# Two layers of a hybrid backbone on one core: value-weight sums in other memory, modulation in fourteen couples, a shorter plan for the first merge

## The chip, the cores and the metric

The kernel runs on one core of a Trainium2 chip. The time is that of the device in microseconds, a median of runs. The engines are TensorE (PE, its weight loads PEld), VectorE (DVE), ScalarE (ACT), GpSimd (POOL) and SyncE (SP), which here only issues DMAs. They run their own programs and meet at semaphores.

## The reference

Two layers work on 256 latent tokens and 256 context tokens of width 1024, all in float32. Cut to what the change touches:

```python
mod_x = s_c @ w_ada[l] + b_ada[l]             # modulation: six vectors of 1024, for tokens and for context
hx = rms_norm(x, norm1_g[l]) * (1 + scx1) + shx1
px = hx @ w_in[l]                             # one combined projection: r k v ... of RWKV, q k v of attention, mLSTM, gates
ya, yb, yc = rwkv_mix(...), na_mix(...), mlstm_mix(...)
merged = ga * (ya @ w_branch[0]) + gb * (yb @ w_branch[1]) + gc * (yc @ w_branch[2])
x = x + gx1 * (merged @ w_out)
x = x + gx2 * moe_ffn(...)                    # 64 experts, 8 of them for each token
```

`wkv_scan` in the RWKV mixer is a recurrence over tokens; the kernel computes it in chunks of 64 tokens and in both directions.

## The kernel before

The stages of a layer run one behind the other, each in its own block, which ends when all engines are through: start or combine, projection (`stage_projection`), attention, mLSTM, RWKV features, scan (`stage_rwkv_scan`), readout, merge (`stage_merge`), norm, experts. SP issues the loads of a stage in a written order.

**Projection.** The weights come in 10 blocks of 1024x512 through a ring of two (`win_ring`). A block holds two couples of tiles. A couple of tiles times all 512 tokens is done by seven products of half size (Strassen's scheme in Winograd's form) where plain products would be eight: `PRODUCTS` is their order, p1, p2, p6, p7, p4, p5, p3. A product is four matmuls of 128x256 in the code, eight records in the trace; PE goes on through six PSUM banks (`NB` in the first layer; `free` waits until a bank is read). Left operands are sums of weight tiles (`left_sums`, four DVE instructions of 128x512, two sets kept in `left`), right ones sums of the activations (`right_sums`, four of 128x1024, in `right`). p1 and p2 need no sums; PE waits for them ahead of the third product (L716 to L721). Blocks 8 and 9 hold the value weights of attention and mLSTM, whose result is wanted with tokens on the partitions: there the roles turn, the token tiles are the left side (`token_sums`, eight instructions, into `token`) and the weights the right one (`feature_sums`, four instructions, into `right` for block 8 and into `left`'s room for block 9). DVE also adds the products (L834 to L852), seven adds a couple. ScalarE copies p1 (L747).

In the first layer the projection also computes eight blocks of modulation on DVE (`accumulate`, L778): a piece is one of the eight row tiles of a 1024x512 block, two instructions of 128x512 (context and token vector) and a drain, 64 pieces in all. The 16 couples of blocks 0 to 7 (`by_weights`) take four pieces each: one third behind p2's add, one behind p7's, the rest at the couple's end behind the left sums (L857). The weights of modulation alternate between `token`'s room and that of `vna` and `vml` (`halves`). When a block is summed, PE folds it with `modulate` (L686) a couple later, ScalarE copies a row, PE turns it (`turn`, L695) and DVE writes it into `k.mod` (`finish`). `acc` holds the sums of two blocks. The order of DVE's work in couple 15, after its adds: its last pieces, `token_sums`, `feature_sums(8)` (L859 to L862).

**Scan.** For each direction d there are four PSUM banks. At the start PE transposes the values, 128 tokens at a time (`values`, L2093), into bank 2 (`psV`), ScalarE copies them out (L1872), and PE waits for all four copies (L2232) ahead of `matrices`, which write banks 0, 1 and the second half of 2 (L2104, L2109). DVE copies them under a mask (`first_factor` L2013, `masks` L2034); POOL has to have cleared and filled the target first (`filled`, L1953, L1955). Then come the levels of a blockwise inverse (`level`). Bank 3 (`psR`, `psU`, `psY`) is first written inside level 1.

**Merge.** For each of the eight column tiles m, PE computes three gate products (those not done ahead) and three branch products; DVE multiplies and adds them into `mg`; behind that come eight output products (L2565). In the first layer the twelve modulation blocks of the second layer are computed in the gaps: `merge_plan` (L2363) lays down at fixed costs which pieces DVE does behind each tile and behind which product PE does `modulate` and `turn` of a block. Blocks turned ahead of the output products (`in_loop`, here 9) use the banks of `psO`, the others those of `psG`; so the first output product waits for `finish` of the last of them (L2561).

Of the kernel before, what the change touches and what calls it, by code (L numbers as in the profile page):

```python
# [16 lines left out]
ALU = mybir.AluOpType  # L17
# [517 lines left out]
def right_sums(dve, out, b):  # L535

    dve.tensor_tensor(out[:, 0], b(0, 1), b(0, 0), ALU.subtract)
    dve.tensor_tensor(out[:, 2], b(1, 1), b(0, 1), ALU.subtract)
    dve.drain()
    dve.tensor_tensor(out[:, 1], b(1, 1), out[:, 0], ALU.subtract)  # L540
    dve.drain()
    return dve.tensor_tensor(out[:, 3], out[:, 1], b(1, 0), ALU.subtract)


def operands_of(name, a, left, b, right):

    return {"p1": (lambda: (a(0, 0), b(0, 0))), "p2": (lambda: (a(0, 1), b(1, 0))), "p3": (lambda: (left[:, 3], b(1, 1))),
            "p4": (lambda: (a(1, 1), right[:, 3])), "p5": (lambda: (left[:, 0], right[:, 0])),
            "p6": (lambda: (left[:, 1], right[:, 1])), "p7": (lambda: (left[:, 2], right[:, 2]))}[name]()


def stage_projection(nc, k, l, h, pr, pn, vna, vml):
# [40 lines left out]
    per_unit = -(-NA * KD // len(by_weights))  # L593
    summed_in = [by_weights[(KD * (a + 1) - 1) // per_unit] for a in range(NA)]

    with ExitStack() as ctx:
# [20 lines left out]

        def ada_part(a, c):
            return halves[a % 2][c // HK][:, c % HK]
# [13 lines left out]
        def sides(u):  # L633

            pair, j, m = units[u]
            if j < 8:
                return w_tile(j, m), left[:, pair_of[u] % 2], h_part, right
            return h_tile(m), token[:, m // 2], w_part(j), right if j == 8 else right9
# [13 lines left out]
        with nc.Block(no_gpsimd_drain=True) as block:  # L652
# [103 lines left out]
            def _(dve):  # L756
# [16 lines left out]
                def feature_sums(j):  # L773
                    dve.wait_ge(win_in[j % 2].sem, win_in[j % 2].at(j // 2 * 16 + 16))
                    dve.wait_ge(done.sem, done.at(first_done[by_weights[-1]] + 7))
                    right_sums(dve, right if j == 8 else right9, w_part(j)).then_inc(rights.sem, 1)
# [32 lines left out]
                right_sums(dve, right, h_part).then_inc(rights.sem, 1)  # L809
# [11 lines left out]
                for u, (pair, j, m) in enumerate(units):  # L821
                    p, q, n = pair_of[u], first_done[u], 4 * j + m
                    if pair:
                        own, one = tmp[:, p % 2], p1[:, p % 2]
                        pieces = [p * per_unit + i for i in range(per_unit)] if j < 8 else []
# [33 lines left out]
                        if NA and u == by_weights[-1]:  # L859
                            token_sums()  # L860
                        if u == by_weights[-1]:
# [911 lines left out]
def stage_rwkv_scan(nc, k, l, pr, pn, sg, aa, kk, ka, y, h):  # L1773
# [21 lines left out]
    with ExitStack() as ctx:  # L1795
# [31 lines left out]
        psV = [ps[d][:, 2] for d in range(2)]  # L1827
# [26 lines left out]
        with nc.Block(no_gpsimd_drain=True) as block:  # L1854
# [230 lines left out]
            def _(pe):  # L2085
# [74 lines left out]
                def between(d, n, m):  # L2160
# [4 lines left out]
                    elif m == 1:  # L2165
                        w(pe, d, "state", n)
                        pe.wait_ge(sem[d]["yout"].sem, sem[d]["yout"].at(y_read(n)))
# [64 lines left out]
                pe.wait_ge(values_out.sem, values_out.at(NV))  # L2232
# [130 lines left out]
def merge_plan(blocks, m0):  # L2363
# [3 lines left out]
    for m in range(KD):  # L2367
# [4 lines left out]
        for b in range(3):  # L2372
            now += BRANCH
            hooks.append((now, ("branch", m, b)))
# [6 lines left out]
    on_pe = {at: [] for _, at in hooks + [last]}  # L2381
# [1312 lines left out]
```

## Time and profile before

| | |
|---|---|
| median of the runs | 2557.25 us (3 runs, 2554.91 to 2565.0) |
| the profiled execution | 2556.32 us, span 2554.5 us |
| PE busy | 2233.2 us, 87% |
| PE weight loads busy | 1587.9 us, 62% |
| DVE busy | 1292.5 us, 51% |
| ACT busy | 674.9 us, 26% |
| POOL busy | 406.9 us, 16% |

The first projection lies from 42 to 308 us of the span, the first scan from 534, the first merge's last branch products around 905 and its output products from 913; the second layer's scan begins at 1882. Busy time doesn't count semaphores and branches. A row of the timeline is a run of like instructions, and the brackets name the idle time ahead of it and what ended it. The granted clock is a share of 2.4 GHz: 1.00 is that level, 0.50 is 1.2 GHz.

### The profile page before, as it was taken

To read this page: it belongs to the slowest core of one execution; us is meant where nothing else is said; L and a number is where in the kernel's file an instruction comes from. 1 tells how busy PE (TensorE), PEld (TensorE's weight loads), DVE (VectorE), ACT (ScalarE), POOL (GpSimd) and SP (SyncE) were. 2 spreads that over 40 slices of the span, in tenths; PEclk is the share of its full clock that TensorE was granted. 3 is DMA by queue.
4 is the path that set the end of the run, shared out by engine and by line. 5 is a ranking of instruction groups with operands and counts; after the bars stand their busy time and mean duration, and the time that the engine had idled before them with its cause. 6 is when DMAs were issued, how large, how long until landed. Compare 5 with 4: busy or idle time off the path is not lost. (4 is left out here: it accounts for less than half of the span.)

```text
span 2554.5 us, 47659 instructions
## 1 busy us (share of the span) xinstructions
PE 2233.2 (87%) x18986; PEld 1587.9 (62%) x18986; DVE 1292.5 (51%) x2881; ACT 674.9 (26%) x1533; POOL 406.9 (16%) x489
## 2 busy tenths in 40 slices
PE   6999889889899998898898589999879978888885
PEld 4887765458844444565565578877658867655453
DVE  5888364676558876442122653344667532531113
ACT  2000155454430003132222110034454431122220
POOL 0000000235500001232221000000234400222210
PEclk9999999999999998999999899999989998898998
DMA  8443001100067524899896822222310052899994
GB/s 353 164 166 132 34 1 60 75 35 4 4 233 282 175 93 167 320 419 398 348 359 234 358 111 99 99 76 94 104 33 4 4 211 101 348 414 376 384 380 174
DMA packets 83245, 474.31 MB, mean 186 GB/s; under 512 B 17617, under 2 KB 29521, under 8 KB 52049
## 3 DMA queue, kind: packets, MB, share of 16 engines
q1 hardware_dynamic: 54704, 394.66, 39.6%
q0 software_dynamic: 28320, 76.60, 8.1%
q8 instruction: 153, 2.51, 0.4%
q14 instruction: 68, 0.55, 0.1%
HBM read 439.99 MB, written 61.08 MB: 196 GB/s over the span
## 5 line engine op out<-in xcount | busy, mean ns | idle before, releaser
L3007 PE MATMUL xp_psG<-moe_ring,rt_xt 128*64 128x256 f32 (+1 forms) x2048 | 331.3, 410 | 42.7 <-DMA moe_ring<-in_moe 38.8
L3007 PEld LDWEIGHTS xp_psG<-moe_ring,rt_xt 128*64 128x64 f32 (+1 forms) x2048 | 228.6, 165 | 123.4 <-issue 63.1
L3264 DVE TENSOR_TENSOR rt_sg<-rt_sg,xp_psG 128x128 f32<-128x128 f32 x84 | 24.2, 288 | 356.7 <-ACT rt_sg L3081 356.7
L3028 PE MATMUL xp_psY<-moe_ring,rt_aT 128*64 128x512 f32 (+1 forms) x512 | 161.9, 602 | 1.6 <-DVE rt_aT L3271 1.6
L724 PE MATMUL win_ps<-win_right,win_left 128*128 128x256 f32 x600 | 138.0, 380 | 2.3 <-DVE win_left L532 2.3
L724 PEld LDWEIGHTS win_ps<-win_right,win_left 128*128 128x128 f32 x600 | 113.7, 190 | 19.0 <-DVE win_left L532 2.7
L1223 POOL MEMSET ml_w<- 128x1536 f32 x4 | 5.4, 1376 | 736.4 <-POOLq L922 736.4
L2619 DVE SCALAR_TENSOR_TENSOR pr<-pr,cv_silu 128x512 f32<-128x512 f32 x168 | 118.7, 748 | 4.9 <-DMA pr<-in_ada 0.6
L2139 PE MATMUL sc_ps<-sc_NT,sc_XI 64*64 64x64 f32 x2560 | 109.4, 227 | 9.1 <-DVE sc_XI L2019 4.8
L3075 ACT ACTIVATE rt_xt<-xp_psT 128x512 f32<-128x512 f32 x168 | 90.9, 595 | 95.2 <-PE xp_psT L2992 95.1
L2134 PE MATMUL sc_ps<-sc_XI,sc_NT 64*64 64x64 f32 x2048 | 106.6, 227 | 6.2 <-issue 3.0
L2881 POOL DMA_INDIRECT y_rows<-rt_y,rt_dst x56 | 56.1, 1002 | 300.5 <-PE xp_psT L2992 207.2
L2019 DVE TENSOR_TENSOR sc_XI<-sc_ps,cst 128x256 f32<-128x256 f32 x160 | 67.5, 422 | 71.0 <-PE sc_ps L2139 69.5
L3081 ACT ACTIVATE rt_sg<-xp_psG 128x128 f32<-128x128 f32 x84 | 23.3, 277 | 288.8 <-PE xp_psG L3007 288.8
L2992 PEld LDWEIGHTS xp_psT<-cst,rt_xg 128*128 128x128 f32 x512 | 58.1, 143 | 63.9 <-issue 35.2
L724 PE MATMUL win_ps<-h,win_ring 128*128 128x256 f32 x400 | 93.0, 386 | 5.4 <-PEq L292 5.4
L2134 PEld LDWEIGHTS sc_ps<-sc_XI,sc_NT 64*64 64x64 f32 x2048 | 82.8, 135 | 18.7 <-issue 9.3
L3028 PEld LDWEIGHTS xp_psY<-moe_ring,rt_aT 128*64 128x64 f32 (+1 forms) x512 | 51.7, 153 | 66.7 <-issue 60.7
L2139 PEld LDWEIGHTS sc_ps<-sc_NT,sc_XI 64*64 64x64 f32 x2560 | 85.9, 134 | 11.3 <-DVE sc_XI L2019 6.3
L2565 PE MATMUL mg_psO<-mg_m,mg_wo 128*128 128x512 f32 (+1 forms) x256 | 85.6, 493 | 5.3 <-DVE scratch L2636 3.5
L1878 ACT ACTIVATE sc_NT<-sc_ps 128x256 f32<-128x256 f32 x160 | 61.4, 384 | 106.6 <-PE sc_ps L2139 104.8
L2992 PE MATMUL xp_psT<-cst,rt_xg 128*128 128x128 f32 x512 | 69.9, 281 | 21.1 <-DMA rt_xg<-h_rows,rt_tok 21.1
(551 smaller groups left out, 4569.3 us busy)
## 6 DMA issues: line engine op xcount, KB each, us to landing
moe_ring<-in_moe SPq DMA_DIRECT2D x128, 1536.0 KB, 14.1
win_ring<-in_win SPq DMA_DIRECT2D x20, 2048.0 KB, 8.2
pr<-in_ada POOLq DMA_DIRECT2D x24, 1024.0 KB, 5.6
cb_yg<-y_rows SPq DMA_DIRECT2D x16, 1024.0 KB, 11.8
mg_ring<-in_mg SPq DMA_DIRECT2D x16, 768.0 KB, 4.5
win_token<-in_ada SPq DMA_DIRECT2D x8, 1024.0 KB, 7.9
mg_wo<-in_wo SPq DMA_DIRECT2D x2, 4096.0 KB, 15.0
pr<-y_rows SPq DMA_DIRECT2D x8, 1024.0 KB, 17.7
```

Source lines behind the costliest of these rows:

```text
L724: last = pe.matmul(ps[:, (q + f) % NB, 0:256], x[:, c], y[:, c], start=c == 0, stop=c == HK - 1)
L1878: act.activation(NT[d][:], psWT[d], ACT.Copy).then_inc(sem[d]["wtout"].sem, 1)
L2019: dve.tensor_tensor(XI[d][:], psW[d], level_mask(d, m), ALU.mult).then_inc(sem[d]["xi"].sem, 1)
L2134: pe.matmul(psW[d][to:to + HD, hp], wt, x, start=True, stop=True)
L2139: last = pe.matmul(out[to:to + HD], x, wt, start=True, stop=True)
L2565: last = pe.matmul(psO[:, m % 2, 0:N], wo[:, c, m * P:(m + 1) * P], mg[:, c, t0:T], start=c == 0, stop=c == KD - 1)
L2619: last = dve.scalar_tensor_tensor(out=acc[:, a % 2, s], in0=slot[:, c], scalar=weight, in1=acc[:, a % 2, s], op0=ALU.mult, op1=ALU.add)
L2881: pool.indirect_dma_start(k.d_y[0:N * TOP_K], bass.IndirectOffsetOnAxis(ap=dst[:, column(u)], axis=0), y_rows[u % OUT], None, bounds_check ...
L2992: last = pe.transpose(psT[:, u % 2, c], xg[u % AHEAD][:, c * P:(c + 1) * P], k.cst("ident"))
L3007: last = pe.matmul(psG[at:at + m, u % 2, 0:2 * P].rearrange("p (q n) -> p q n", q=2), xt[:, u % 2, c, at:at + m], ring[:, slot, c:2 * KD:K ...
L3028: last = pe.matmul(psY[at:at + m, q], aT[:, u % 2, at:at + m], ring[:, slot, 2 * KD + 4 * q:2 * KD + 4 * q + 4], start=True, stop=True)
L3075: last = act.activation(xt[:, u % 2, q * 4:q * 4 + 4], psT[:, u % 2, q * 4:q * 4 + 4], ACT.Copy)
```

## The change

It has three parts. First, the 64 pieces of modulation go to the first 14 couples (4 or 5 each, `shares`) and none to couples 14 and 15, so that blocks are summed in couples 1, 3, 5, 6, 8, 10, 12 and 13 where it was every second couple to 15. In the first layer the right sums of block 8 are written to the room of `acc` and of the front of `vml` (`right8`) and not to `right`; they wait for the last `modulate` (`ada_done`) and not for couple 15's products. The token sums stand behind couple 14's work, the feature sums of block 8 behind couple 15's. Second, in the scan of both layers `psV` is bank 3, and the wait for the four copies stands ahead of the first write of bank 3 in level 1. Third, in `merge_plan` the branch products of the last column tile carry no modulation. Worked out with the plan's own costs, in the first layer modulate and turn of block index 8 move from the last tile's first and second branch product to output products 0 and 1, those of 9, 10 and 11 each one product later (turn of 11 to output product 7), `in_loop` becomes 8, `finish(8)` moves from behind the last column tile to behind output product 1. The second layer's merge has no modulation and stays as it is.

```diff
--- before.py
+++ after.py
@@ -534,19 +534,19 @@
-    dve.tensor_tensor(out[:, 0], b(0, 1), b(0, 0), ALU.subtract)
-    dve.tensor_tensor(out[:, 2], b(1, 1), b(0, 1), ALU.subtract)
+    dve.tensor_tensor(out[0], b(0, 1), b(0, 0), ALU.subtract)
+    dve.tensor_tensor(out[2], b(1, 1), b(0, 1), ALU.subtract)
     dve.drain()
-    dve.tensor_tensor(out[:, 1], b(1, 1), out[:, 0], ALU.subtract)
+    dve.tensor_tensor(out[1], b(1, 1), out[0], ALU.subtract)
     dve.drain()
-    return dve.tensor_tensor(out[:, 3], out[:, 1], b(1, 0), ALU.subtract)
+    return dve.tensor_tensor(out[3], out[1], b(1, 0), ALU.subtract)
...
     return {"p1": (lambda: (a(0, 0), b(0, 0))), "p2": (lambda: (a(0, 1), b(1, 0))), "p3": (lambda: (left[:, 3], b(1, 1))),
-            "p4": (lambda: (a(1, 1), right[:, 3])), "p5": (lambda: (left[:, 0], right[:, 0])),
-            "p6": (lambda: (left[:, 1], right[:, 1])), "p7": (lambda: (left[:, 2], right[:, 2]))}[name]()
+            "p4": (lambda: (a(1, 1), right[3])), "p5": (lambda: (left[:, 0], right[0])),
+            "p6": (lambda: (left[:, 1], right[1])), "p7": (lambda: (left[:, 2], right[2]))}[name]()
@@ -590,8 +590,9 @@
-    per_unit = -(-NA * KD // len(by_weights))
-    summed_in = [by_weights[(KD * (a + 1) - 1) // per_unit] for a in range(NA)]
+    EARLY = 14
+    shares = [range(NA * KD * i // EARLY, NA * KD * (i + 1) // EARLY) if i < EARLY else range(0) for i in range(len(by_weights))]
+    summed_in = [by_weights[next(i for i, x in enumerate(shares) if KD * (a + 1) - 1 in x)] for a in range(NA)]
@@ -615,6 +616,14 @@
+        if NA:
+            flat_acc = acc[:].rearrange("p a s n -> p (a s n)").rearrange("p (f c n) -> p f c n", f=2, c=HK)
+            flat_vml = vml[:].rearrange("p a h v -> p (a h v)")[:, 0:HK * 512].rearrange("p (f c n) -> p f c n", f=2, c=HK)
+            right8 = [flat_acc[:, 0], flat_acc[:, 1], flat_vml[:, 0], flat_vml[:, 1]]
+        else:
+            right8 = [right[:, f] for f in range(4)]
+        early = NA > 0
+
         def ada_part(a, c):
@@ -634,8 +643,8 @@
             if j < 8:
-                return w_tile(j, m), left[:, pair_of[u] % 2], h_part, right
-            return h_tile(m), token[:, m // 2], w_part(j), right if j == 8 else right9
+                return w_tile(j, m), left[:, pair_of[u] % 2], h_part, [right[:, f] for f in range(4)]
+            return h_tile(m), token[:, m // 2], w_part(j), right8 if j == 8 else [right9[:, f] for f in range(4)]
@@ -772,8 +781,11 @@
                     dve.wait_ge(win_in[j % 2].sem, win_in[j % 2].at(j // 2 * 16 + 16))
-                    dve.wait_ge(done.sem, done.at(first_done[by_weights[-1]] + 7))
-                    right_sums(dve, right if j == 8 else right9, w_part(j)).then_inc(rights.sem, 1)
+                    if j == 8 and early:
+                        dve.wait_ge(ada_done.sem, ada_done.at(NA))
+                    else:
+                        dve.wait_ge(done.sem, done.at(first_done[by_weights[-1]] + 7))
+                    right_sums(dve, right8 if j == 8 else [right9[:, f] for f in range(4)], w_part(j)).then_inc(rights.sem, 1)
@@ -806,7 +818,7 @@
-                right_sums(dve, right, h_part).then_inc(rights.sem, 1)
+                right_sums(dve, [right[:, f] for f in range(4)], h_part).then_inc(rights.sem, 1)
                 weight_sums(0)
@@ -822,7 +834,7 @@
                         own, one = tmp[:, p % 2], p1[:, p % 2]
-                        pieces = [p * per_unit + i for i in range(per_unit)] if j < 8 else []
+                        pieces = list(shares[p]) if j < 8 else []
                         a, b = len(pieces) // 3, 2 * len(pieces) // 3
@@ -856,9 +868,11 @@
                             accumulate(i)
-                        if NA and u == by_weights[-1]:
+                        if early and u == by_weights[-2]:
                             token_sums()
-                        if u == by_weights[-1]:
+                        if early and u == by_weights[-1]:
+                            feature_sums(8)
+                        if not early and u == by_weights[-1]:
                             feature_sums(8)
@@ -1824,7 +1838,7 @@
         psA2 = [[half(d, 2, 1)[o * HD:(o + 1) * HD] for o in range(2)] for d in range(2)]
-        psV = [ps[d][:, 2] for d in range(2)]
+        psV = [ps[d][:, 3] for d in range(2)]
         psBK = [ps[d][:, 2] for d in range(2)]
@@ -2164,6 +2178,8 @@
                         w(pe, d, "state", n)
+                        if n == 0:
+                            pe.wait_ge(values_out.sem, values_out.at(NV))
                         pe.wait_ge(sem[d]["yout"].sem, sem[d]["yout"].at(y_read(n)))
@@ -2229,7 +2245,6 @@
                     values(j)
-                pe.wait_ge(values_out.sem, values_out.at(NV))
                 for d in range(2):
@@ -2371,14 +2386,15 @@
             now += BRANCH
-            hooks.append((now, ("branch", m, b)))
+            if m < KD - 1:
+                hooks.append((now, ("branch", m, b)))
         ends.append(now)
...
     last = (now + 3.0, ("end", 0, 0))
-    on_pe = {at: [] for _, at in hooks + [last]}
+    on_pe = {at: [] for _, at in hooks + [last] + [(0.0, ("branch", KD - 1, b)) for b in range(3)]}
     turned = []
...
```

## Rows read from the trace of the kernel before

**Rows 1.** What PE waited for, one of its rows: us in total, times, longest.

```profile
PE win_ps L724 <- DVE win_right L542: 10.6, 1, 10.6
```

**Rows 2.** Timeline of PE at block 8: start us, us, engine, line, operation.

```profile
245.84 3.62 PE L724 MATMUL win_ps<-win_ring,h 128*128 128x256 f32 x16
260.00 5.49 PE L724 MATMUL win_ps<-win_right,win_token 128*128 128x256 f32 x16 [10.55 <-DVE win_right L542]
```

**Rows 3.** Timeline of DVE in the same stretch.

```profile
246.27 2.89 DVE L792 SCALAR_TENSOR_TENSOR win_acc<-vml,cv_silu,win_acc 128x512 f32<-128x512 f32 x4
...
254.90 1.22 DVE L537 TENSOR_TENSOR win_right<-win_ring 128x1024 f32<-128x1024 f32 x1
```

**Rows 4.** Windows: busy time (and instructions) by engine, granted clock, DMA share, GB/s.

```profile
260.00:264.00 4.00, 4.00 (x10) 3.25 (x11) 0.69 (x3) 0.00 (x0) 0.00 (x0) 0.54 0.02 4
...
912.70:915.40 2.70, 2.64 (x3) 1.17 (x4) 1.24 (x2) 0.00 (x0) 0.00 (x0) 0.50 0.00 0
```

**Rows 5.** Timeline of PE behind two other idles, projection and second merge.

```profile
49.44 3.72 PE L724 MATMUL win_ps<-win_right,win_left 128*128 128x256 f32 x16 [2.33 <-DVE win_left L532]
...
2131.54 27.86 PE L2565 MATMUL mg_psO<-mg_m,mg_wo 128*128 128x256 f32 x128 [1.77 <-DVE mg_m L2658]
```

**Rows 6.** Projection, couples 3 to 12: window, DVE's waits, starts of couples.

```profile
104.60:214.20 109.60, 109.60 (x574) 94.23 (x573) 96.28 (x196) 4.84 (x14) 0.00 (x0) 1.00 0.47 173
...
DVE pn L852 <- PE win_ps L724: 4.4, 5, 1.0
DVE pr L852 <- PE win_ps L724: 1.3, 2, 1.0
...
95.52 3.62 PE L724 MATMUL win_ps<-h,win_ring 128*128 128x256 f32 x16
...
120.68 3.62 PE L724 MATMUL win_ps<-h,win_ring 128*128 128x256 f32 x16
...
95.61 0.42 DVE L852 TENSOR_TENSOR pr<-win_ps,win_tmp 128x256 f32<-128x256 f32 x1 [0.97 <-PE win_ps L724]
...
104.64 0.42 DVE L834 TENSOR_TENSOR pr<-win_ps,win_p 128x256 f32<-128x256 f32 x1
...
115.91 0.42 DVE L834 TENSOR_TENSOR pr<-win_ps,win_p 128x256 f32<-128x256 f32 x1
```

**Rows 7.** Timeline of the first layer's scan from its start.

```profile
536.62 2.33 PE L2093 MATMUL sc_ps<-cst,pr 128*128 128x128 f32 x8 [0.66 <-ACT sc_uv L1872]
540.27 2.08 PE L2104 MATMUL sc_ps<-sc_ra,sc_hat 64*128 64x128 f32 x16 [1.32 <-ACT sc_uv L1872]
...
537.85 0.61 DVE L1940 TENSOR_TENSOR sc_hat<-sc_kd,sc_rise 128x256 f32<-128x256 f32 x1
...
541.50 0.62 DVE L1940 TENSOR_TENSOR sc_hat<-sc_kd,sc_rise 128x256 f32<-128x256 f32 x1
543.52 0.90 DVE L2013 COPY_PREDICATED pn<-cst,sc_ps 64x256 f32<-64x256 uint32 x2 [1.41 <-PE sc_ps L2109]
```

**Rows 8.** Timeline of the second layer's scan.

```profile
1893.72 1.42 POOL L1953 COPY h<-cst 64x256 f32<-64x256 f32 x4 [8.73 <-issue]
...
1895.40 0.89 DVE L2013 COPY_PREDICATED pn<-cst,sc_ps 64x256 f32<-64x256 uint32 x2 [6.63 <-POOL scratch L1955]
```

**Rows 9.** Timeline of the first layer's merge, last branch products and output products.

```profile
905.67 3.60 PE L2548 MATMUL mg_psY<-pn,mg_ring 128*128 128x512 f32 x8
912.76 15.38 PE L2565 MATMUL mg_psO<-mg_m,mg_wo 128*128 128x512 f32 x32 [3.49 <-DVE scratch L2636]
928.07 0.62 PE L2510 MATMUL mg_psG<-pr,mg_pick 128*2 128x128 f32 x16
928.61 7.13 PE L2565 MATMUL mg_psO<-mg_m,mg_wo 128*128 128x512 f32 x16
...
935.69 7.03 PE L2565 MATMUL mg_psO<-mg_m,mg_wo 128*128 128x512 f32 x16
...
910.92 0.69 DVE L2658 TENSOR_TENSOR mg_m<-mg_gateb 128x512 f32<-128x512 f32 x1
```

## The prediction

> **What bounds the kernel now.** I read the engine shares first (the table above), then what TensorE (PE) waited for, then the timelines around the three places that the change touches. PE is busy for most of the span, but a share doesn't price an edit: the stages run one behind the other, so a stage gets shorter only where PE, or the chain that feeds it, waits less. PE's waits in reach of the diff are 10.6 us before the third product of the first projection's block 8 [rows 1], 3.5 us before the first output product of the first layer's merge [rows 9], and 1.3 us in the first layer's scan before the first matrices [rows 7]. Of the rest nothing is edited but the like place in the second layer's scan. The prize is below 20 us, and the question is how much of each wait another wait takes over.
>
> **Part A, the first projection.** 64 pieces of modulation go into 14 couples of tiles instead of 16 (4 or 5 a couple, none in the last two), and the sums for block 8 (the token sums, and `feature_sums(8)` into `right8`) move ahead.
>
> What is removed. After the last add of couple 15, VectorE (DVE) does two pieces (246.27), then the token sums, then the four feature sums (254.90) [rows 3]. PE does block 8's first two products, which need no sums, until 245.84+3.62=249.46 and goes on at 260.00, 10.55 us idle [rows 2]. In the changed kernel pieces and token sums are gone from here, and the feature sums start at 246.27, right behind the same add. From their first start to PE's go they take 260.00-254.90=5.10 us, so PE goes on at 251.37 after 1.91 us: 8.64 gained. The late one is again the feature sums: they still stand behind couple 15's adds in DVE's program, though the ring's block 8 and `ada_done` (the eighth modulation, now after couple 14) are there. That modulation and its turn cost PE about 0.65 us (in the merge the like take 928.61-928.07 and 0.1, [rows 9]); they move from behind block 8's products to ahead of them, both ends of the sum shift alike, and it is neither cost nor gain.
>
> The clock. Behind the 10.55 us of idleness the granted clock was 0.54, mostly the 1.2 GHz level, for 4 us [rows 4]; the two products took 5.49 us where the two ahead of the idle took 3.62 [rows 2]: 1.87 lost. Idles of 2.33 and 1.77 us were followed by matmuls at the 2.4 GHz level (16 in 3.72 us, 128 in 27.86) [rows 5]; 3.5 us in the merge were followed by 0.50 [rows 4]. The new idle of 1.9 us lies between the two that cost nothing, so I count all of 1.87 as gained; bounds 0 and 1.87.
>
> What is added. DVE gets 8 pieces more ahead of couple 14. Two pieces' four instructions take 2.89 us [rows 3], with the drain 1.49 a piece. In couples 4 to 12 (109.6 us) DVE waited at least 5.7 us for PE, and the plan puts 41-36=5 pieces more there, 7.5 us: the waits are used up and DVE falls back up to 2 us more. Does PE feel it? DVE starts couple 4's adds at 104.64, 9.1 us behind PE's start on it at 95.52 [rows 6]. PE has six PSUM banks, so it needs a couple's fourth add three products into the next couple. Two couples take it 120.68-95.52=25.16 us, modulation included [rows 6], so that is 12.6+5.2=17.8 us after its start on this one. With a lag of 9.4 and three pieces ahead of that add, it is done after about 15.8. So the cover is some 2 us; beyond it each microsecond of lag costs PE one. The left sums are tighter in one place: those of couple 4 can start only in couple 3, whose middle third gets one piece more; 1.49 less the 0.97 that DVE waited before the add at 95.61 [rows 6] leaves 0.5 us, and PE now comes right behind them: 0.5 lost. The SP queue keeps its order; three of the modulation loads go out one or two couples earlier, and the loads of weights stand behind none that waits for later work than theirs. Part A: -8.64-1.87+0.5=**-10.0 us**, bounds -8.1 and -10.5.
>
> **Part B, the scans.** The transposed values go to PSUM bank 3, and PE's wait for ScalarE's copies moves behind level 0, to the first other write of that bank. In the first layer PE's matrices start at 540.27, released by the copies, while DVE has the first factors at 537.85+0.61=538.46 and PE's transposes end at 536.62+2.33=538.95 [rows 7]. They can start 1.3 to 1.4 us earlier. Next late are DVE's own operands for direction 1, which end at 541.50+0.62=542.12, against 543.52 at which DVE now starts on the masks [rows 7]: 1.4 us is also the most that DVE can give. The second direction's matrices, 16 of which take 2.08 us at the start [rows 7], then have to be there when DVE has done 2.2 us of masks, and may be up to 0.9 late. Taken -1.2, bounds -0.5 and -1.4. In the second layer DVE starts the masks only at 1895.40, released by GpSimd, whose copies began at 1893.72 after 8.73 us for which no wait is shown [rows 8]. PE's being earlier changes nothing there: 0. Part B: **-1.2 us**.
>
> **Part C, the first merge.** The last column's branch products carry no modulation any more: modulate and turn of the ninth block move to the output products, `in_loop` becomes 8 instead of 9, and the first output product waits for `finish(7)`, done long before, and not for `finish(8)`. Now the last branch product ends at 905.67+3.60=909.27, DVE multiplies, adds, and writes the merged tile from 910.92 to 911.61, then clears a bank and finishes the ninth block; PE starts at 912.76 [rows 9]. Without the finish it would start at 911.7. The modulation taken out (0.65) makes the whole chain that much earlier, 911.1, and the same is paid later among the output products: net 1.05. The first two output products took 928.07-912.76=15.31 us where two take 14.06 [rows 9]: 1.25 for the clock, 0.50 at first [rows 4]. The new idle is 911.1-908.6=2.5 us, just above the 2.33 that cost nothing and below the 3.5 that cost; I take it as free, bounds 0 and 1.25. Behind it PE always has work: DVE needs per output product at most four pieces and two adds, 6.9 us in 7.03, with one product of slack, and the last turn falls under DVE's last two adds. Part C: **-2.3 us**, bounds -1.0 and -2.3.
>
> **Sum.** -10.0-1.2-2.3=-13.5 us. The profiled execution took 2556.3 (its span of 2554.5 and 1.8 around it), 0.9 below the median of 2557.25. So 2542.8 for it and **2543.7 us** as a median, 0.53% less. A measurement of this kernel can tell about 0.5%, 12.8 us, from no change: the forecast lies just beyond that line.
>
> **Rivals.**
> 1. The clock falls behind one of the two short idles. For it: 2.5 us is beyond every idle that was free in the rows. Against: 2.33 was free. It gives back 1.25 or 1.87, both 3.1: 2545.0 to 2546.8. Chance 0.12.
> 2. DVE already paces PE in the projection. Then the 8 pieces brought forward (11.9 us) lengthen it by what they save: part A is near 0, the total about -3.5 to -5, 2552 to 2554. For it: DVE is busy for 96.3 of 109.6 us there. Against: PE shows no idle in that window, and DVE waits for PE [rows 6]. Chance 0.09. The Trainium skill (Trainium Kernel Development and Optimization, Best Practices) asks to judge by the weight loads' share and not by matmul busy time. By that PE isn't full in this window (94.2 of 109.6 us), which would speak for this rival; the rows bear it out only so far as no release by DVE stands ahead of a matmul there.
> 3. A wait without a shown cause, like GpSimd's 8.73 us, goes or comes. Gone in the second scan, DVE could start up to 6.6 us earlier: 2536 to 2537.5, chance 0.05. A new one on a chain that counts: 2546 to 2552, chance 0.07.
> 4. It doesn't do what it says, because the feature sums find another late input (the ring's block 8, loaded at the end of couple 13): 2549 to 2552, chance 0.03.
> 5. Slower: DVE's backlog in the projection. Couple 4 takes DVE 11.3 us with four pieces (104.64 to 115.91, [rows 6]), so 12.1 with the mean of 4.57, against PE's 12.6. The change loses as soon as the 11 couples from 3 to 13 overrun by more than 13.5/11=1.2 us each, which is a couple of 13.8 us or a piece of 1.86 us instead of 1.49. At 2.5 us a piece it is 4.1 over in each, 45 us less 13.5 won: near 2590. Chance 0.04.
>
> The forecast's own case has 0.60: 2541 to 2546 with the runs' scatter, 0.43 of it below 2544.5 and 0.17 above. Faster 0.43+0.05=0.48; same 0.17+0.12+0.09+0.07+0.03=0.48; slower 0.04. Range: 2539 to 2551; it leaves out the vanished wait, rival 2 and the slower one.
>
> **What would show it.** A: a PE idle of about 2 us before block 8's third product, full clock behind it; DVE nearly without waits in couples 3 to 13 and no PE idle there beyond 0.5. B: the first scan's masks 1.2 to 1.4 us nearer to the stage's start, the second's unchanged. C: a PE idle near 2.5 us before the output products, ended by the merged tile. Wrong: PE waits for left sums or adds between couples 5 and 13, a clock of 0.50 after either short idle, or another stage of other length.

## The result, and the profile after

The changed kernel takes 2547.15 us, the median of 7 runs (2541.5 to 2550.54); the kernel before took 2561.01 beside it (2554.91 to 2565.0, 7 runs). The ratio is 0.9944, with a 95% interval of 0.9927 to 0.9961: 13.9 us less, 0.56%. A second set of the same two kernels gave 0.9938 (0.992 to 0.9955). The profiled execution of after has a span of 2544.0 us, before's had 2554.5. Its page begins, busy time by engine:

```profile
PE 2239.1 (88%) x18986; PEld 1594.4 (63%) x18986; DVE 1292.5 (51%) x2881; ACT 675.8 (27%) x1533; POOL 407.7 (16%) x489
```

DVE has 1292.5 us of work as before, 5.9 us more stand for PE: nothing was saved in work, the gain is in waits.

Lines behind the edits have moved: in the projection L724 is L733, L834 to L852 are L846 to L864; in the scan L1940, L2013 and L2104 are L1954, L2027 and L2118; in the merge L2565 and L2658 are L2581 and L2674.

Timeline of PE in after at block 8 (start us, us, engine, line, operation, count; in brackets the idle ahead of it and what ended it), against [rows 2]:

```profile
246.24 3.62 PE L733 MATMUL win_ps<-win_ring,h 128*128 128x256 f32 x16
251.77 2.56 PE L733 MATMUL win_ps<-win_acc,win_token 128*128 128x256 f32 x8 [1.91 <-DVE vml L542]
254.12 3.03 PE L733 MATMUL win_ps<-vml,win_token 128*128 128x256 f32 x8
256.99 1.89 PE L733 MATMUL win_ps<-vml,h 128*128 128x256 f32 x8
```

The wait is 1.91 us where it was 10.55. But the two products behind it take 2.56 and 3.03 us where the same work takes 1.89 a little later. The windows of 10 us behind the wait, in before, after and after's twelve-couple sister further below (us, busy time of PE, PEld, DVE, ACT and POOL, granted clock, DMA share, GB/s):

```profile
260.00:270.00 10.00, 9.99 (x38) 8.53 (x39) 2.57 (x8) 0.00 (x0) 0.00 (x0) 0.82 0.01 2
```

```profile
251.77:261.77 10.00, 10.00 (x39) 8.51 (x40) 2.57 (x8) 0.00 (x0) 0.00 (x0) 0.83 0.12 52
```

```profile
259.05:269.05 10.00, 10.00 (x46) 8.82 (x47) 3.37 (x9) 0.00 (x0) 0.00 (x0) 1.00 0.11 46
```

The first two are alike: the clock fell to its 1.2 GHz level behind 1.91 us of idleness as it had behind 10.55. The third had 2.02 us of idleness and kept 2.4 GHz.

Timeline of DVE in after ahead of that wait, against [rows 3]:

```profile
246.33 0.42 DVE L864 TENSOR_TENSOR pn<-win_ps,win_tmp 128x256 f32<-128x256 f32 x1 [0.97 <-PE win_ps L733]
246.67 1.22 DVE L537 TENSOR_TENSOR win_acc<-win_ring 128x1024 f32<-128x1024 f32 x1
...
250.40 1.23 DVE L542 TENSOR_TENSOR vml<-win_acc,win_ring 128x1024 f32<-128x1024 f32 x1
```

The sums for block 8 start right behind couple 15's last add. No wait took the removed one's place; the window from couple 4 to the end of couple 15, against the one in [rows 6]:

```profile
102.50:246.24 143.74, 143.74 (x758) 123.46 (x758) 127.17 (x262) 6.17 (x18) 0.00 (x0) 1.00 0.38 145
```

PE is busy in all of it. DVE, which waited for PE at least 5.7 us in couples 4 to 12 of before, has from 102.50 to 221 us only two idles of 0.4 us, and none of them for PE.

The scans and the merge, timelines of DVE, POOL and PE in after, against [rows 7], [rows 8] and [rows 9]. The first scan's stage starts at 526.68 (before: 533.99), the second's at 1871.13 (before: 1881.88); a stage starts here with the first load that it issues, the scan with POOL's first clearing.

```profile
534.74 0.89 DVE L2027 COPY_PREDICATED pn<-cst,sc_ps 64x256 f32<-64x256 uint32 x2
...
1882.98 1.43 POOL L1967 COPY h<-cst 64x256 f32<-64x256 f32 x4 [8.73 <-issue]
1884.66 0.89 DVE L2027 COPY_PREDICATED pn<-cst,sc_ps 64x256 f32<-64x256 uint32 x2 [6.63 <-POOL scratch L1969]
...
902.89 7.11 PE L2581 MATMUL mg_psO<-mg_m,mg_wo 128*128 128x512 f32 x16 [2.60 <-DVE mg_m L2674]
```

The masks of the first scan come 8.06 us behind the stage's start, where they came 9.53 behind it; those of the second come 13.53 behind, where it was 13.52. The first output product waits 2.60 us for the merged tile instead of 3.49 for the finish, and takes 7.11 us, full speed.

Length of the stages in the two profiles, in us. Stages that differ by less than 0.6 are left out:

| stage | before | after | edited |
|---|---|---|---|
| start | 41.66 | 41.04 | no |
| projection, layer 1 | 266.93 | 258.36 | part A |
| attention, layer 1 | 75.37 | 78.12 | no |
| scan, layer 1 | 171.06 | 169.27 | part B |
| merge, layer 1 | 243.28 | 241.85 | part C |
| experts, layer 1 | 412.50 | 410.09 | no |
| projection, layer 2 | 210.28 | 209.66 | no |
| mLSTM and features, layer 2 | 119.37 | 122.04 | no |
| scan, layer 2 | 170.40 | 171.57 | part B |

The edited stages of the first layer give 11.8 us; unedited ones move by up to 2.8 us in either direction. The experiments had to say whether those belong to the change.

### The profile page after: what moved, and what is told of

The parts are those of the page before. It is cut to its first block and busy times, and to the rows that moved or that the text cites. A ratio compares the mean times of both kernels' runs of the same rounds, so it can differ in the third digit from the quotient of the medians.

```text
span 2544.0 us, 47659 instructions
## 1 busy us (share of the span) xinstructions
PE 2239.1 (88%) x18986; PEld 1594.4 (63%) x18986; DVE 1292.5 (51%) x2881; ACT 675.8 (27%) x1533; POOL 407.7 (16%) x489
## 5 line engine op out<-in xcount | busy, mean ns | idle before, releaser
L733 PE MATMUL win_ps<-win_right,win_left 128*128 128x256 f32 x600 | 138.0, 380 | 2.3 <-DVE win_left L532 2.2
L733 PEld LDWEIGHTS win_ps<-win_right,win_left 128*128 128x128 f32 x600 | 113.7, 190 | 19.1 <-DVE win_left L532 2.6
L733 PE MATMUL win_ps<-h,win_ring 128*128 128x256 f32 x400 | 93.2, 387 | 5.4 <-PEq L292 5.4
L2581 PE MATMUL mg_psO<-mg_m,mg_wo 128*128 128x512 f32 (+1 forms) x256 | 84.4, 488 | 4.4 <-DVE mg_m L2674 4.4
L733 PEld LDWEIGHTS win_ps<-h,win_ring 128*128 128x128 f32 x400 | 76.2, 193 | 17.8 <-issue 7.3
```

Of the source, the lines that this page charges most:

```text
L733: last = pe.matmul(ps[:, (q + f) % NB, 0:256], x[:, c], y[:, c], start=c == 0, stop=c == HK - 1)
L2581: last = pe.matmul(psO[:, m % 2, 0:N], wo[:, c, m * P:(m + 1) * P], mg[:, c, t0:T], start=c == 0, stop=c == KD - 1)
```

## Experiments

The theory: the three parts add up, each by the wait it shortens; what is left in the projection is the last 1.9 us and the clock behind it. Rivals: DVE is close to pacing the projection; the longer attention is a price of part A. The first four kernels ran beside 24 runs of before (median 2561.95), the next four beside 29 (2560.93), the last four beside 17 (2563.21).

### Each part alone

`a_alone` is before with the new `stage_projection` and its helpers. `b_alone` is before with the scan's edit:

```diff
-            psV = [ps[d][:, 2] for d in range(2)]
+            psV = [ps[d][:, 3] for d in range(2)]
...
+                        if n == 0:
+                            pe.wait_ge(values_out.sem, values_out.at(NV))
...
-                pe.wait_ge(values_out.sem, values_out.at(NV))
```

`c_alone` is before with the merge's plan:

```diff
-            hooks.append((now, ("branch", m, b)))
+            if m < KD - 1:
+                hooks.append((now, ("branch", m, b)))
```

> The projection part alone: fourteen couples, the sums for block 8 in the other memory, scan and merge as before. My theory (each part pays in its own stage and nothing else is moved): the projection stage takes 266.9 us less 8.4 to 10.2, that is 256.7 to 258.5, with a PE idle of 1.9 us before block 8's third product; the low end when the clock stays at 1.00 behind it, the high end when it falls as in the profile of after. Whole time 8 to 10.5 us below before. Rival (VectorE paces the projection): PE waits for sums or adds in couples 4 to 13 and the stage takes 262 us or more; whole time less than 5 us below.

> The scan part alone: values transposed into bank 3, their wait behind level 0. Theory: the first layer's masks start 8.1 us behind the stage's start and not 9.5, the second layer's 13.5 as before, since GpSimd's copies come 8.7 us late there. Whole time 1.5 us below before, which the timing can't tell from none. Rival (the second layer gains too, in time though not at the masks): 3 us.

> The merge plan alone. Theory: PE idles 2.5 us and not 3.5 before the first output product, ended by the merged tile, the last branch products carry 0.65 us less, and the first merge is 1.0 to 2.3 us shorter, the latter when the clock stays at 1.00. Whole time 1 to 2.3 us below before. Rival (the gain is given back among the output products, where one more fold and turn stand and VectorE is nearly full): PE waits there and the stage is the same to 0.3 us.

| | median us | ratio to before, 95% | projection | scan 1, to the masks | merge, layer 1 |
|---|---|---|---|---|---|
| a_alone | 2552.0 | 0.9968 (0.995 to 0.9985) | 258.34 | 9.54 | 243.87 |
| b_alone | 2558.14 | 0.9995 (0.9979 to 1.0011) | 267.93 | 8.14 | 244.01 |
| c_alone | 2559.08 | 0.9989 (0.9977 to 1.0001) | 266.94 | 9.54 | 242.19 |

By these ratios, taken of 2561 us, that is -8.2, -1.3 and -2.8 us, together -12.3, and after had by the same reckoning -14.3 and -15.9 in its two sets. (The medians of this set differ by 10.0, 3.8 and 2.9 us; a single set doesn't say more closely than that.) B and C alone can't be told from no change by the run times; their places in the profile can. Each part moves its own place and not the others'. Over all fourteen profiles of this study the first scan's stage takes 170.3 us on average with part B (9 profiles) and 172.3 without (5), and the first merge 241.7 with part C (9) and 243.7 without (5). A single pair says less: the first scan took 171.06 and 173.58 us in the two profiles of before, so part B is read from the masks' place and not from the stage's length.

In b_alone the clock behind the 10.5 us of idleness was lower for longer than in before, 0.72 over the ten microseconds where before had 0.82:

```profile
260.57:270.57 10.00, 10.00 (x34) 8.29 (x35) 1.84 (x7) 0.00 (x0) 0.00 (x0) 0.72 0.01 2
```

Nothing is edited there, and the stage is 1.0 us longer: the clock's return alone makes that much scatter.

### The last 1.9 us: sums inside the last couple

`split` moves the four sums for block 8 from behind couple 15's last add to between its adds, where DVE waited for PE anyway:

```diff
+                        if early and u == by_weights[-1]:
+                            feature_sums(8)
                         dve.tensor_tensor(home(j, n + 1, 0), shaped(own[:, 1], n), shaped(product("p4"), n), ALU.subtract
...
-                        if early and u == by_weights[-1]:
-                            feature_sums(8)
```

> The changed kernel with one thing more: the feature sums of block 8 stand in the middle of couple 15's adds (behind p7's), where VectorE waits 3.6 us for PE, and not behind them. Theory (those sums are what PE waits 1.9 us for, and the clock falls for that idle in part of the executions): no PE idle before block 8's third product, clock 1.00 there, the projection stage 2 to 3.9 us shorter than in after (258.4 in its profile), so 254.5 to 256.4; whole time 2 to 4 us below after. Rival (couple 15's later adds now stop PE at its banks): a PE idle within the first five products of block 8, and no gain or a loss up to 2 us.

```profile
250.13 1.89 PE L733 MATMUL win_ps<-win_acc,win_token 128*128 128x256 f32 x8
251.85 1.89 PE L733 MATMUL win_ps<-vml,win_token 128*128 128x256 f32 x8
...
242.17 1.22 DVE L537 TENSOR_TENSOR win_acc<-win_ring 128x1024 f32<-128x1024 f32 x1 [0.16 <-issue]
...
247.05 0.41 DVE L859 TENSOR_TENSOR pn<-win_tmp,win_ps 128x256 f32<-128x256 f32 x1
```

PE's and DVE's timelines of split. The idle is gone, and the products behind it take 1.89 us each, the clock at 1.00. The projection takes 254.51 us, 3.85 less than after: 2.08 up to the third product, and 1.77 from there to the stage's end (47.63 us in after, 45.86 in split), which is the clock. The run times: 2544.98 us, ratio 0.9932 (0.9913 to 0.9952). In the second set:

> The kernel after, unchanged: ratio 0.9944 within 0.0017. Projection 258.4, first scan 8.1 us to its masks, merge wait 2.6. The attention of the first layer, which gave back 2.75 us of the projection's 8.57 in the first profile: 78.1 again if the change's projection leads to it, 75 to 77.5 if it was scatter.

> The kernel that makes block 8's right sums between the last couple's adds, beside the kernel after on the same chip now. Its first profile had no wait before block 8's third product and no fall of the clock, and a projection of 254.51 against after's 258.36. Theory (the remaining 1.9 us of wait and the clock's fall behind it cost 3.85 us): 3.9 us less than after in the medians, ratio to before 0.9929; rival (the projection's gain is given back in the attention, which took 78.3): ratio as after's, 0.9944.

after_again: 2546.48 us, 0.9938 (0.992 to 0.9955). split_again: 2545.38 us, 0.994 (0.9922 to 0.9959), with a projection of 254.52 in its profile beside 258.35. So the projection's 3.8 us are there each time, while the medians differ by 1.1 in this set. Each interval reaches some 4.5 us to either side, and can't tell 1 from 3.8: in the profiles the gain is shown, in the run times it isn't.

### What the clock costs, with the idle filled

`fill` is before, with 47 unused matmuls ahead of the third product of block 8, where PE waited:

```diff
                             if f == 2:
+                                if NA and j == 8 and m == 0:
+                                    for c in range(47):
+                                        pe.matmul(psA[:, 256:512], h_tile(0)(0, 0)[:, c % HK], w_part(8)(0, 0)[:, c % HK],
+                                                  start=True, stop=True)
```

> The kernel before, with 47 unused products of 128 by 256 columns put on TensorE ahead of the third product of block 8, where it waited 10.55 us: at 0.216 us each (1.73 us between starts of eight) they fill 10.2 us of the wait. No other work is moved, and the wait for DVE's sums stays as long. If the clock behind the wait is a price of the idle, it stays at 1.00 there and the projection's stage takes 1.9 us less than before's 266.93 (265.1); if the clock fell for another reason (transfers, DVE's work), the stage stays at 266.9. Second question: with the change's first part, the attention of the first layer took 78.1 us in three profiles and without it 75.4 to 77.3, though nothing in it is edited. If it takes that from how its start lies to the clock's falls and not from the edit, it may come out anywhere from 75 to 78.5 here; if a granted clock without a fall at 250 to 260 us leads to the longer half-clock stretch in the attention, it is 78 here as well. Whole kernel: -2 us against before by the first theory alone, 0 with the attention's 2.7 us given back.

My count was wrong: a matmul of 256 columns in the code is two records of 0.216 us, so the 47 take twice the time that I wrote. Timeline of PE in fill:

```profile
249.15 20.45 PE L718 MATMUL win_psA<-win_ring,h 128*128 128x256 f32 x94
269.44 3.62 PE L728 MATMUL win_ps<-win_right,win_token 128*128 128x256 f32 x16
```

PE goes on 9.4 us later than in before, the stage takes 274.65 us, and the kernel 2563.48 (ratio 1.0013, 1.0 to 1.0026). The question is answered all the same, by the stretch from the third product to the stage's end: 48.59 us in before (260.00 to 308.59), 46.72 in fill (269.44 to 316.16), with the clock at 1.00. The difference is 1.87 us, what [rows 2] gave for the clock. What is between fill's 46.72 and split's 45.86 is the fold and turn of the eighth modulation, which the change has moved ahead: 0.86 us.

### How near DVE is to pacing the projection

`twelve` and `ten` are after with the modulation in twelve and in ten couples:

```diff
-    EARLY = 14
+    EARLY = 12
```

> The kernel after, with the modulation's 48 pieces in twelve couples (4 each) in place of fourteen (3 or 4). The profile after has a DVE step of 10.9 to 13.6 us a couple, 12.5 on average, and PE has no wait in couples 3 to 13. A piece is 1.50 us, so DVE would take 0.57 x 1.50 = 0.86 us more a couple, in twelve couples some 10 us, before two couples with none. If DVE is about to pace the projection (rival 2), PE gets waits before the sums of the left operands or for free banks: what lies beyond the cover of about 3 us, 3 to 7 us in all. If DVE has room, the projection stays within 0.5 us of after's 258.4 and PE shows no idle row before 246 us.

> As the one with twelve, with 4.8 pieces in each of ten couples: 1.37 x 1.50 = 2.1 us more a couple for DVE, 21 us over ten. If DVE then paces PE, the projection takes 10 to 18 us more than after's 258.4 and loses all that the change gained (total near or above before's); PE's idle rows lie in couples 3 to 10 and their releaser is DVE. If DVE has room in its waits alone, the loss is under 3 us.

Both expectations count 48 pieces; there are 64, so 4.57 a couple in after, 5.33 in twelve and 6.4 in ten. With 1.49 us a piece and 12.1 us a couple in after that is 13.2 and 14.8 us for DVE against PE's 12.6. Timeline of PE in ten (the two rows ahead) and in twelve, rows with an idle:

```profile
77.25 5.31 PE L733 MATMUL win_ps<-win_right,win_left 128*128 128x256 f32 x16 [2.41 <-DVE win_left L532]
...
161.75 1.97 PE L733 MATMUL win_ps<-h,win_ring 128*128 128x256 f32 x8 [1.32 <-DVE win_tmp L850]
```

```profile
89.41 3.69 PE L733 MATMUL win_ps<-win_right,win_left 128*128 128x256 f32 x16 [1.05 <-DVE win_left L532]
164.83 1.97 PE L733 MATMUL win_ps<-h,win_ring 128*128 128x256 f32 x8 [0.79 <-DVE win_tmp L850]
```

twelve has six such rows between the first couples and block 8, 3.60 us in all, and a projection of 261.93 us, 3.57 more than after. The two numbers are near each other by chance: from the stage's start to block 8's third product twelve took 215.99 us where after took 210.73, 5.26 more, and behind it 45.94 instead of 47.63, because its clock stayed up. The 1.55 us beyond the waits and the 0.11 by which the last idle is longer no row shows as a wait of PE. Part of it stands at the waits: where PE goes on, the row behind one of 1.89 us starts 1.73 us behind its start, so six waits cost some 0.16 us more each, an estimate from these rows. The kernel takes 2554.59 us (0.9971, 0.9958 to 0.9985). ten has eleven, 12.3 us, and a projection of 276.36, 18.0 more; the kernel takes 2563.67 (1.0021, 1.0005 to 1.0038) and has lost the whole gain. The waits are of the two kinds that the prediction named, for the left sums and for a free bank, but for one of 1.54 us in ten ahead of a turn. So fourteen couples is the edge: PE has no wait, and 0.76 pieces more a couple would give it some.

ten shows one thing more. Its waits are 12.3 us, its stage is 18.0 longer. Of the rest 3.3 us are the clock, which fell behind idles of 2.41 and 2.62 us: the products behind them take 5.31 and 5.38 us instead of 3.72. Windows of 10 us from 77.25 and 107.69:

```profile
77.25:87.25 10.00, 10.00 (x39) 8.57 (x40) 9.34 (x17) 0.00 (x0) 0.00 (x0) 0.84 0.57 241
107.69:117.69 10.00, 10.00 (x39) 8.52 (x40) 9.30 (x20) 0.00 (x0) 0.00 (x0) 0.83 0.52 190
```

### The attention: a price of the change, or scatter

The first layer's attention has no edit, and took 2.75 us longer in after's profile, in a_alone's and (2.9) in split's. That looked like a price of part A. The answer is in a second profile of before:

> The kernel before, unchanged. It gives a second profile of the same code and the distance between two sets of runs of one kernel. Ratio 1.000 within 0.0015. If what the unedited stages of the profiles differ by (attention of the first layer 75.4 to 79.4 us, its mLSTM stage's sister in the second layer 61.4 to 64.5, the expert stage of the first layer 409 to 415) is scatter of an execution, this profile differs from the first in them by the same amounts: over 1 us in at least two. If each kernel has its own values, they are within 0.5 us of before's first profile (75.37, 61.39, 412.50), and the edits would have set the others. The edited places stay: projection 266.9 (10.55 us of wait), scan 9.5 us to its masks, merge wait 3.5.

before_again: 2561.66 us, ratio 0.9993 (0.9978 to 1.0008). The windows are the first 30 us of the attention's stage in, from above, before, before_again, after, split and split_again:

```profile
308.59:338.59 30.00, 22.07 (x127) 15.21 (x127) 17.15 (x36) 19.09 (x44) 0.00 (x0) 0.83 0.20 71
```

```profile
308.64:338.64 30.00, 23.16 (x94) 15.62 (x95) 14.98 (x30) 16.76 (x37) 0.00 (x0) 0.61 0.19 70
```

```profile
299.40:329.40 30.00, 23.17 (x105) 15.63 (x105) 16.01 (x33) 17.82 (x40) 0.00 (x0) 0.66 0.19 70
```

```profile
295.99:325.99 30.00, 23.17 (x103) 15.63 (x103) 16.00 (x33) 17.81 (x40) 0.00 (x0) 0.66 0.19 70
```

```profile
297.05:327.05 30.00, 22.04 (x127) 15.18 (x127) 17.14 (x36) 19.09 (x44) 0.00 (x0) 0.83 0.20 71
```

The attention took 75.37, 79.46, 78.12, 78.29 and 75.38 us in these five. One code gives 75.4 and 79.5, another 78.3 and 75.4: the expectation that each kernel has its own value has fallen, and with it the price of part A. What differs is how long PE runs at 1.2 GHz there: 10.2 us in before, c_alone and split_again, 17.1 in b_alone, ten and twelve, 20.5 in after, after_again, a_alone and split, 23.9 in before_again and fill. Over the five kernels' profiles without part A the stage takes 77.4 us on average, over the seven with it also 77.4 (those with the unused matmuls below are left out). The experts' stage of the first layer is as loose: 412.50 and 409.56 in the two profiles of before, 408.8 to 415.4 over all fourteen.

PE has an idle of 4.00 us in this stage, and it is tempting to call it the cause. Timeline of PE and a quarter of a microsecond in before_again:

```profile
312.88 4.79 PE L1051 MATMUL na_psO<-cst,na_qsq 128*128 128x2 f32 x32
321.67 2.08 PE L1062 MATMUL na_psS<-pn 64*128 64x256 f32 x8 [4.00 <-ACT na_rq L954]
...
315.14:315.39 0.25, 0.25 (x3) 0.25 (x3) 0.00 (x0) 0.00 (x0) 0.00 (x0) 0.50 0.47 197
```

The clock was at 0.50 there 2.5 us before that idle began (at 317.67), while PE was busy with matmuls of 2 columns. In before_again and fill it fell 6.5 us behind the stage's start and in b_alone and ten 7.3 us, all ahead of the idle, which begins there 7.9 us behind the start or later; in the other eight (again without those with the unused matmuls) it fell 8.0 to 9.7 us behind the start, within the idle.

### Unused products in the attention

`split_attention` is split with six unused matmuls of 512 columns in PE's idles ahead of and behind the first scores:

```diff
+                if l == 0:
+                    for c in range(4):
+                        pe.matmul(psT[:, 0].rearrange("p j n -> p (j n)"), k.cst("blk"), ksq[:, c], start=True, stop=True)
                 pe.wait_ge(rq_done.sem, rq_done.at(1))
                 scores(0)
                 scores(1)
+                if l == 0:
+                    for c in range(2):
+                        pe.matmul(psT[:, 0].rearrange("p j n -> p (j n)"), k.cst("blk"), ksq[:, c], start=True, stop=True)
```

> The split kernel, with six unused products of 128 by 512 columns in the first layer's attention: four in TensorE's 4.00 us of idle before the scores, two in the 2.14 us behind them. In the split kernel's profile the clock is at half for 20.5 us from there, with PE busy in most of it. If that fall is the price of these idles, the clock stays at 1.00 and the attention takes 5 to 8 us less than split's 78.29 (before's, with 10.5 us at half clock, took 75.37, so 2.8 us for 10 us less of it): 71 to 73 us, and the whole -5 to -7 us against split. If the fall has another cause, or if ACT and DVE pace the attention, it stays at 77 to 79 us, or gets up to 0.5 us longer where the unused products delay the scores.

> The split kernel with the six unused products in the attention, beside the split kernel on the same chip now. Its first profile had a half-clock stretch of 4 us in the attention in place of 20.5, and an attention of 74.62 in place of 78.29. Theory: 3.7 us less than split in the medians, ratio about 0.9915; rival (what the attention gains is lost in later stages or in the scatter): as split, 0.993.

Timeline of PE and the first 30 us of the stage in split_attention:

```profile
301.47 3.63 PE L1065 MATMUL na_psO<-cst,na_qsq 128*128 128x2 f32 x32
304.96 5.38 PE L1120 MATMUL na_psT<-na_ksq,cst 128*128 128x512 f32 x8
...
297.23:327.23 30.00, 27.21 (x145) 17.24 (x146) 17.82 (x38) 19.75 (x47) 0.00 (x0) 0.94 0.19 71
```

The stage takes 74.62 us in both profiles of this kernel. Neither case of the first expectation came, 71 to 73 us with the clock held or 77 to 79 without: the clock still fell, 8.8 us behind the stage's start as in split, though PE had work without a gap by then; but it came back after 3.4 us instead of 10.2 to 23.9. So the 4 us of idle aren't needed for the fall, as before_again had shown. What stood ahead of it was 1.50 us of idleness at the stage's start, 3.7 us of wide matmuls and 3.63 us of matmuls with 2 columns. The gain is 3.7 us against the long stretch and 0.8 against the short one. In run times: 2540.49 us (0.9924, 0.9905 to 0.9943), and in the set beside split_again 2545.7 (0.9931, 0.991 to 0.9952) against 2545.38. The second expectation, 3.7 us less than split in the medians, did not come: the profiles show the gain, the medians don't separate the two kernels.

## Why the prediction was right, point by point

I predicted 2543.7 us against a median of 2557.25, 13.5 less; measured were 13.9 less, at 2547.15. The 3.4 us between the two times are the base: the three runs that I had lay 3.8 us low (2557.25 against 2561.01 beside the changed kernel, and 2560.9 to 2563.2 in later sets). The forecast's own part is the difference. The bound of 0.5% was met by the median (0.56%) and not by the whole interval.

**Part A: forecast -10.0 with bounds of -8.1 and -10.5, measured -8.57 in the profile (-8.2 by a_alone's ratio).** The idle was forecast at 1.91 us and is 1.91, so 8.64 gained. **The step that failed is the clock**: "The new idle of 1.9 us lies between the two that cost nothing, so I count all of 1.87 as gained". Of the 1.87, 1.77 were paid again. The price itself was right, fill and split measured 1.87 and 1.77. Wrong was to read the length of an idle as what decides. What happened at block 8 is rival 1, which had 0.12; the forecast's own case, with 0.60, wanted full clock there. Behind about 2 us of idleness before block 8 the clock fell in four of five profiles (after, after_again, a_alone, ten) and not in twelve, behind 2.60 us in the merge it fell in one of nine, behind 2.33 [rows 5], and behind the 1.34 to 2.33 us at the same place in the other thirteen, it didn't. The left sums of couple 4 were forecast at 0.5 lost. From the stage's start to the third product, 7.61 us were gained, 8.47 with the 0.86 of modulation that was moved ahead, against the idle's 8.64: 0.17 lost. That shift of 0.86 I had at 0.65; it is neither cost nor gain, as the prediction said.

**Part B: forecast -1.2, measured -1.47 in after (-1.39 in b_alone and split).** The bound of 1.4 was a little tight. The second layer's 0 holds: GpSimd's 8.73 us stood in every profile that I read for it, so rival 3's vanishing wait did not show.

**Part C: forecast -2.3, measured -2.0 on average** (1.43 between the first profiles of before and after, and before's was the shortest of its five). The idle was forecast at 2.5 us and is 2.60, ended by the merged tile as forecast. The first output product starts on average 1.4 us nearer to the stage's start, where 1.7 were forecast (1.05 and the 0.65 of modulation that moves behind it); the output products give the other 0.6, as forecast. The clock stayed at 2.4 GHz in eight of nine profiles with this edit. The ninth, after_again:

```profile
905.45 8.80 PE L2581 MATMUL mg_psO<-mg_m,mg_wo 128*128 128x512 f32 x16 [2.60 <-DVE mg_m L2674]
```

8.80 us for what took 7.11. Rival 1's price for the merge, 1.25, is 1.69 where it comes.

**Rivals 2 and 5, DVE paces.** They fell for fourteen couples: PE has no wait there. That DVE's time a couple is what counts is borne out by twelve: with 13.2 us a couple against 12.6 PE waited for left sums and for free banks. An overrun of 0.6 us in some nine couples and 3.6 us of waits fit the cover of "some 2 us" that the prediction worked out; that is an estimate, the cover itself wasn't measured. Rival 2 was near.

**Rival 4** fell: the feature sums start behind the last add with no other input late.

**The sum.** -8.57-1.47-2.0 is -12.0 us; the whole runs gave -14.3 and -15.9 by their ratios, with intervals of 4 to 5 us to each side, so the sum of the places is within them; what the 2 to 4 us between them are stays open. That the sum agreed to 0.4 us with the first median is in part luck: the clock's 1.77 us are missing from my forecast, and the rest lies within what unedited stages scatter by.

**The signs of being wrong.** The prediction named three, and two came: a clock of 0.50 behind a short idle, and an unedited stage of another length (the attention, 2.75 us, which the second profile of before shows to be scatter). The third, PE waiting for left sums or adds between couples 5 and 13, did not.

## What to carry to other kernels

A wait whose two ends are both in the trace can be forecast to 0.1 us by moving the rows; what another wait or the clock does behind it can't, and gets a range instead of a value. Before an unedited stage's other length is put down to an edit, take a second profile of the unchanged kernel: here it removed a price of 2.75 us that three profiles seemed to show. And where an engine has waits inside the last step before a stall, put the stalled work there: that gave what spreading the work evenly left over.

## What the runs showed of the hardware

- The clock's fall is not decided by the length of the idle ahead alone. About 2 us ahead of block 8 cost 1.8 us in four profiles and nothing in one, and 1.34 to 2.33 us at the projection's start cost nothing in fourteen; 2.60 us cost nothing in eight and 1.69 in one; some 3.5 us cost in all five where it stood. In the attention the clock fell in six profiles while PE was busy, in four of them with matmuls of 2 columns. The Trainium skill (TensorE: Matmul & The Clock Gate, "What's actually happening") says that the point at which activity is judged runs free of the kernel's start, so that one kernel counts different numbers of half-rate products from run to run. It says so of a kernel's start; the two profiles of before show the like inside a kernel: one code, 10.2 and 23.9 us at 1.2 GHz in the same stage.
- Unused matmuls in PE's idle of 10.55 us ahead of block 8 kept the clock at 1.00 (one profile, fill). In the attention they did not keep it up, but brought it back sooner: 3.4 us at 1.2 GHz in both profiles with them, 10.2 to 23.9 in the twelve without. Which feature of the work ahead makes it fall stays open.
- A float32 matmul in the code is two records of 0.216 us for 256 columns; a time per record must not be multiplied by a count in the code.
